# The compression of keys and values in steps beside the projection columns of the second block's attention

## The reference

```python
parts = jnp.split(h @ w_kv, 6, axis=-1)           # kc, vc, ks, vs, kw, vw: 4 groups x 64 each
kc, ks, kw = rope(kc, pos), rope(ks, pos), rope(kw, pos)
def compress(t, pe, w1, w2):                      # 15 blocks of 32 tokens, stride 16
    blk = t[:, cidx] + pe[None, None, :, None, :]
    blk = blk.transpose(0, 3, 1, 2, 4).reshape(B, G, n_cmp, CMP_LEN * dh)
    return jax.nn.gelu(blk @ w1) @ w2             # w1: 2048 x 256, w2: 256 x 64
k_cmp = compress(kc, cmp_pe_k, cmp_k_w1, cmp_k_w2)
v_cmp = compress(vc, cmp_pe_v, cmp_v_w1, cmp_v_w2)
proj = h @ w_in                                   # queries 1024 columns, gates 48
```

## Time and profile before

| | |
|---|---|
| median of three runs | 1549.62 us |
| profiled execution, its own time | 1545.94 us |
| span of its trace | 1544.1 us |
| PE busy | 1411.0 us (91%) |
| DVE busy | 1151.0 us (75%) |
| ACT busy | 930.5 us (60%) |
| chain that ended last | PE 75%, DVE 12%, DMA 5%, ACT 4%, issue 3% |

### The profile page before, as it was taken

The page is one execution under the profiler, slowest core; times in us unless marked ns, Lnnn a source line. Parts: engine busy times, 40 slices in busy tenths (PEclk is TensorE's granted clock), DMA queues, the critical chain, the costliest instruction groups (busy, mean ns, idle before and its releaser), DMA issues.

```text
span 1544.1 us, 18883 instructions
## 1 busy us (share of the span) xinstructions
PE 1411.0 (91%) x7388; PEld 1181.8 (77%) x7388; DVE 1151.0 (75%) x1371; ACT 930.5 (60%) x1094; POOL 77.8 (5%) x80
## 2 busy tenths in 40 slices
PE   6999996999999696799699999996999999699998
PEld 5877875888888585577578888875778887599986
DVE  4775658999999766377689999987567456558772
ACT  4454535989988434055389999873555654445561
POOL 0000000000000000000100000000276000000000
PEclk9999997999999797799699999998999999899999
DMA  9554544999999446200479999993544433545551
GB/s 330 175 163 137 191 163 149 376 388 384 385 400 394 170 142 204 74 1 1 150 266 385 390 386 385 410 375 117 171 141 159 164 137 110 176 149 182 189 178 41
DMA packets 127277, 343.15 MB, mean 222 GB/s; under 512 B 8956, under 2 KB 15692, under 8 KB 110668
## 3 DMA queue, kind: packets, MB, share of 16 engines
q1 hardware_dynamic: 117472, 327.37, 58.4%
q10 hardware_dynamic: 9708, 14.47, 2.9%
HBM read 340.77 MB, written 1.05 MB: 221 GB/s over the span
## 4 chain that ended last, share of the span: by engine, by line
PE 75%; DVE 12%; DMA 5%; ACT 4%; issue 3%; PEldq 1%; PEld 1%; ACTq 0%; DVEq 0%
PE PS L619 24%; PE PS L1248 15%; PE PS L500 8%; PE PS L576 6%; PE PS L556 4%; DVE wlo L467 4%; DMA raw<-in_moe_w_down 2%; PE PS L1287 2%; PE PS L1237 2%; ACT whi L461 2%; DMA raw<-in_moe_w_gate 2%; PE PS L1322 2%; PE PS L1318 1%; PE PS L2016 1%; PE PS L702 1%
## 5 line engine op out<-in xcount | busy, mean ns | idle before, releaser
L467 DVE TENSOR_TENSOR wlo<-raw,whi 128x2048 fp32r<-128x2048 f32 x314 | 707.6, 2277 | 123.8 <-ACT whi L461 118.5
L461 ACT ACTIVATE whi<-raw 128x2048 fp32r<-128x2048 f32 x314 | 589.4, 1897 | 32.0 <-PE PS L556 17.3
L619 PE MATMUL PS<-whi,th 128*128 128x512 f32 (+1 forms) x544 | 217.9, 401 | 6.9 <-DVE tl L717 6.9
L619 PE MATMUL PS<-whi,tl 128*128 128x512 f32 (+1 forms) x544 | 215.9, 397 | 0.0
L619 PE MATMUL PS<-wlo,th 128*128 128x512 f32 (+1 forms) x544 | 214.5, 394 | 0.0
L1248 PE MATMUL PS<-whi,xg 128*128 128x512 f32 x512 | 205.6, 402 | 0.0
L1248 PE MATMUL PS<-wlo,xg 128*128 128x512 f32 x512 | 200.5, 392 | 0.0
L619 PEld LDWEIGHTS PS<-whi,th 128*128 128x128 f32 x544 | 103.7, 191 | 32.4 <-DVE tl L717 7.9
L619 PEld LDWEIGHTS PS<-wlo,th 128*128 128x128 f32 x544 | 103.9, 191 | 23.8
L619 PEld LDWEIGHTS PS<-whi,tl 128*128 128x128 f32 x544 | 103.6, 190 | 23.7
L1248 PEld LDWEIGHTS PS<-whi,xg 128*128 128x128 f32 x512 | 96.4, 188 | 18.6
(11 more groups left out here) (401 smaller groups left out, 2284.2 us busy)
## 6 DMA issues: line engine op xcount, KB each, us to landing
raw<-in_moe_w_gate SPq DMA_DIRECT2D x64, 1024.0 KB, 7.6
raw<-in_moe_w_up SPq DMA_DIRECT2D x64, 1024.0 KB, 8.5
raw<-in_moe_w_down SPq DMA_DIRECT2D x64, 1024.0 KB, 7.9
raw<-in_w_in SPq DMA_DIRECT2D x32, 1024.0 KB, 5.2
raw<-in_ret_w_in SPq DMA_DIRECT2D x24, 1024.0 KB, 5.2
raw<-in_w_up SPq DMA_DIRECT2D x20, 1024.0 KB, 5.1
raw<-in_w_down SPq DMA_DIRECT2D x10, 1024.0 KB, 5.0
raw<-in_ret_w_out SPq DMA_DIRECT2D x8, 1024.0 KB, 5.0
```

Of the source, the lines that this page charges most:

```text
L461: nc.scalar.activation(s.whi[:, high, 0:kc, 0:wide], s.raw[:, slot, 0:kc, 0:wide], ACT.Copy).then_inc(s.hi_done, 1)
L467: nc.vector.tensor_tensor(s.wlo[:, slot, 0:kc, 0:wide], s.raw[:, slot, 0:kc, 0:wide], s.whi[:, high, 0:kc, 0:wide], ALU.subtract).then_inc ...
L619: last = nc.tensor.matmul(PS[:, 2 * (col % 2) + tt, 0:wide], x[:, KC * kb + c, tt * P:(tt + 1) * P], w[:, k, c, 0:wide], start=(kb == 0 an ...
```

## The change

`l_nsa_in` is cut into two query columns (`l_nsa_q`) and a gate column (`l_nsa_g`). Between them stand four new blocks of the ring: the first compression weights, 1024 rows by 256 columns each, loaded by SyncE and used unsplit (ScalarE and VectorE only pass the semaphores on). Sixteen steps stand behind the blocks: 0 to 5 behind keys and values, 6 to 9 behind queries, 10 to 13 behind the compression blocks, 14 and 15 behind the gate blocks. Every column is rotated as soon as it is copied out. The doubled copy goes: VectorE's adds read the transposed tokens in PSUM banks 5 and 6, the lower or upper half of the partitions, and write either half of `cmp_x`. The small compression weights are loaded, in seven transfers issued by ScalarE, ahead of the projection, and GpSimd instead of VectorE sets the zero parts of `n_kp` and `n_vp`. Of the stage ends only the last stays.

```diff
-        l_nsa_in = linear(3, [4, 4], plain(a["nsa_w_in"][0]))
+        l_nsa_q = linear(2, [4, 4], plain(a["nsa_w_in"][0]))
+        cmp_b0 = blocks[0]
+        blocks[0] += 4
+        l_nsa_g = linear(1, [4, 4], plain(a["nsa_w_in"][0], 2 * BW))
...
+        def cmp_sync(sp):
+
+            for i in range(4):
+                b = cmp_b0 + i
+                src = a["cmp_k_w1" if i < 2 else "cmp_v_w1"][D * (i % 2):D * (i % 2) + D, :]
+                sp.wait_ge(block_used, b - RAWS + 1)
+                sp.dma_start(cmp_block(i), src.rearrange("(c p) n -> p c n", p=P)).then_inc(raw_ready[b % RAWS], 16)
+
+        def nsa_split_hi(act, s, b, turn, kc=KC, wide=BW):
+            if cmp_b0 <= b < cmp_b0 + 4:
+                act.wait_ge(raw_ready[b % RAWS], ready_value(s, b, 0))
+                act.drain().then_inc(hi_done, 1)
+            else:
+                split_hi(act, s, b, 0, KC, 3 * NSA_H if l_nsa_g.b0 <= b < l_nsa_g.b0 + 2 else BW)
...
+        def nsa_beside_tensor(pe, n):
+
+            half = CMP_LEN // 2
+            if n == 2:
+                pe.wait_ge(cmp_loaded, 7 * 16)
+                for k in range(2):
+                    for b in range(2):
+                        last = nc.tensor.transpose(PS[:, 4, (2 * k + b) * half:(2 * k + b + 1) * half],
+                                                   cmp_pe[0:half, k, b].rearrange("p a d -> p (a d)"),
+                                                   cst[0:half, C_ID:C_ID + half])
+                last.then_inc(cmp_turned, 1)
+            if n == 3:
+                pe.wait_ge(rotated, ROTATED_KC)
+                for k in range(2):
+                    nsa_turn_tensor(lambda tt: n_kvc[:, tt, :], 256 * k, 5 + k).then_inc(cmp_turned, 1)
+            if n == 7:
+                pe.wait_ge(rotated, ROTATED_KW)
+                pe.wait_ge(cmp_built, BUILT_PE)
+                nsa_turn_tensor(lambda tt: n_k[:, tt, :], 0, 7).then_inc(cmp_turned, 1)
+                nsa_turn_tensor(lambda tt: n_k[:, tt, :], 256, 4).then_inc(cmp_turned, 1)
+            if n == 9:
+                pe.wait_ge(rotated, ROTATED_Q0)
+                pe.wait_ge(cmp_built, BUILT_V)
+                for i in range(2):
+                    last = nsa_turn_tensor(lambda tt: n_q[:, 0, tt, :], 256 * i, 5 + i)
+                last.then_inc(cmp_turned, 1)
+            if n in (12, 14):
+                k = n // 2 - 6
+                pe.wait_ge(cmp_copied, COPIED_GV if k else COPIED_GK)
+                for c in range(2):
+                    last = nc.tensor.transpose(PS[:, 4 if k else 7, 256 + c * 64:256 + c * 64 + 60],
+                                               cmp_g[0:60, k, c * P:(c + 1) * P], cst[0:60, C_ID:C_ID + 60])
+                last.then_inc(cmp_turned, 1)
+            if n == 12:
+                pe.wait_ge(rotated, ROTATED_Q1)
+                pe.wait_ge(cmp_copied, COPIED_Q0)
+                for i in range(2):
+                    last = nsa_turn_tensor(lambda tt: n_q[:, 1, tt, :], 256 * i, 5 + i)
+                last.then_inc(cmp_turned, 1)
+            if n == 13:
+                pe.wait_ge(cmp_built, BUILT_H)
+                for c in range(2):
+                    last = nc.tensor.matmul(PS[:, 7, 384:444], cmp_w2k[:, c, :, :].rearrange("p b d -> p (b d)"),
+                                            cmp_h[:, c, :], start=(c == 0), stop=(c == 1))
+                last.then_inc(cmp_turned, 1)
+            if n == 15:
+                pe.wait_ge(cmp_built, BUILT_HR)
+                for g in range(NSA_G):
+                    for c in range(2):
+                        last = nc.tensor.matmul(PS[0:60, 4, g * NSA_DH:(g + 1) * NSA_DH],
+                                                cmp_hr[:, c, g].rearrange("p r n -> p (r n)"), cmp_w2v[:, c, :],
+                                                start=(c == 0), stop=(c == 1))
+                last.then_inc(cmp_turned, 1)
...
+        def nsa_in_tensor(pe):
+
+            steady_tensor(pe, l_nsa_kv, th, tl, lambda n: nsa_beside_tensor(pe, n))
+            steady_tensor(pe, l_nsa_q, th, tl, lambda n: nsa_beside_tensor(pe, 6 + n))
+            for i in range(4):
+                k = i // 2
+                pe.wait_ge(lo_done, cmp_b0 + i + 1)
+                if i % 2 == 0:
+                    pe.wait_ge(cmp_built, BUILT_KW if k else BUILT_KS)
+                for c in range(8):
+                    last = nc.tensor.matmul(PS[0:60, 4 if k else 7, 0:CMP_HID], cmp_x[:, k, 8 * (i % 2) + c, 0:60],
+                                            cmp_block(i)[:, c, :], start=(i % 2 == 0 and c == 0),
+                                            stop=(i % 2 == 1 and c == 7))
+                last.then_inc(block_used, 1)
+                nsa_beside_tensor(pe, 10 + i)
+            steady_tensor(pe, l_nsa_g, th, tl, lambda n: nsa_beside_tensor(pe, 14 + n))
...
+            if n in (9, 12):
+                j = n // 12
+                act.wait_ge(cmp_turned, (CMP_Q0, CMP_Q1)[j])
+                for i in range(2):
+                    last = nc.scalar.activation(n_qT[:, 4 * j + 2 * i:4 * j + 2 * i + 2, :].rearrange("p c t -> p (c t)"),
+                                                PS[:, 5 + i, :], ACT.Copy)
+                last.then_inc(cmp_copied, 1)
+            if n in (11, 13):
+                k = n // 13
+                act.wait_ge(block_used, cmp_b0 + 2 * k + 2)
+                nc.scalar.activation(cmp_g[0:60, k, :], PS[0:60, 4 if k else 7, 0:CMP_HID],
+                                     ACT.Gelu_apprx_tanh).then_inc(cmp_copied, 1)
...
+        def cmp_build_vector(dve, o, k):
+
+            dve.wait_ge(cmp_turned, (CMP_K, CMP_V)[k])
+            for g in range(NSA_G):
+                rows = slice(64 * (g % 2), 64 * (g % 2) + 64)
+                tokens = PS[rows, 5 + k, SEQ * (g // 2):SEQ * (g // 2) + SEQ].rearrange("p (i s b) -> p s i b", s=8, b=2)
+                for b in range(2):
+                    for h in range(2):
+                        o(nc.vector.tensor_tensor(
+                            cmp_x[64 * b:64 * b + 64, k, 8 * h:8 * h + 8, 15 * g:15 * g + 15], tokens[:, :, h:h + 15, b],
+                            cmp_peT[rows, k, b, 8 * h:8 * h + 8].unsqueeze(2).broadcast_to([64, 8, 15]), ALU.add))
+            o.wait()
+            hand(dve, cmp_built)
+
+        def nsa_beside_vector(dve, o, n):
+
+            if n == 2:
+                dve.wait_ge(cmp_turned, CMP_PE)
+                o.then(nc.vector.tensor_copy(cmp_peT[:, :, :, :].rearrange("p k b s -> p (k b s)"),
+                                             PS[:, 4, 0:2 * CMP_LEN]))
+                hand(dve, cmp_built)
+                o(nc.vector.memset(n_ckp[:, :, :, :], 0.0))
+            if n in (3, 4):
+                cmp_build_vector(dve, o, n - 3)
+            if n == 7:
+                for seg, bank in enumerate((7, 4)):
+                    dve.wait_ge(cmp_copied, (COPIED_KS, COPIED_KW)[seg])
+                    pair = PS[:, bank, :].rearrange("p (c t) -> p c t", c=2)
                     for half in range(2):
...
+        def nsa_rotated(dve, o, l, j, x, heads):
+
+            dve.wait_ge(acc_free, 2 * (l.n0 + j + 1))
+            nsa_rotate(dve, o, x, heads)
+            o.wait()
+            hand(dve, rotated)
+
+        def nsa_in_vector(dve, o):
+
+            def rotate_keys(j):
+                nsa_rotated(dve, o, l_nsa_kv, j, n_kvc if j == 0 else n_k[:, :, 256 * (j - 1):256 * j], 4)
+
+            def rotate_queries(j):
+                nsa_rotated(dve, o, l_nsa_q, j, n_q[:, j], 8)
+
+            def gates_of(j):
+                dve.wait_ge(acc_free, 2 * (l_nsa_g.n0 + 1))
+                nsa_gates_vector(dve, o)
+            steady_side(dve, l_nsa_kv, nsa_split_lo, rotate_keys, lambda n: nsa_beside_vector(dve, o, n))
+            steady_side(dve, l_nsa_q, nsa_split_lo, rotate_queries, lambda n: nsa_beside_vector(dve, o, 6 + n))
+            for i in range(4):
+                nsa_split_lo(dve, sweep_first, cmp_b0 + i + AHEAD, 0)
+                nsa_beside_vector(dve, o, 10 + i)
+            steady_side(dve, l_nsa_g, nsa_split_lo, gates_of, lambda n: nsa_beside_vector(dve, o, 14 + n))
...
+        def cmp_params():
+
+            w2k = a["cmp_k_w2"].rearrange("(c p) d -> p c d", p=P)
+            return [(cmp_pe[0:CMP_LEN // 2, k, :, i, :], a[n].rearrange("(s b) d -> s b d", b=2))
+                    for k, n in enumerate(("cmp_pe_k", "cmp_pe_v")) for i in range(2)] + [
+                (cmp_w2k[:, :, 0, :], w2k), (cmp_w2k[:, :, 1, :], w2k),
+                (cmp_w2v[:, :, :], a["cmp_v_w2"].rearrange("(c p) d -> p c d", p=P))]
...
+                if layer == 0:
+                    pool.wait_ge(normed, 4)
+                    for b in range(2):
+                        o.then(nc.gpsimd.memset(n_kp[64 * b:64 * b + 64, :, :, 1 - b, :], 0.0))
+                    for side in (0, 2):
+                        o.then(nc.gpsimd.memset(n_vp[:, :, :, :, side, :], 0.0))
+                    pool.drain().then_inc(pool_steps, 1)
```

(40 more changed lines are left out.)

275 lines of the change are left out of this document (77 added, 198 removed).

## The result

The changed kernel took 1523.23 us (median of 4 executions, 1517.76 to 1526.32) against 1547.94 before (4 executions, the three shown above among them, 1545.36 to 1552.52): ratio 0.984, 95% interval 0.980 to 0.987. The forecast was 1523, its range 1515 to 1535. The profiled execution took 1521.7 with a span of 1519.9 us; the span before was 1544.1, so the two traces differ by 24.2 us. The changed kernel's trace starts its first projection matmul at 530.62 instead of 531.90, so distances are compared, not times on the axis. My measure is the distance from the first projection matmul of this stage to the first compressed-key score matmul, with which attention opens. Before it was 646.02 - 531.90 = 114.1; now it is 619.96 - 530.62 = 89.3. The gain of 24.8 us lies within this stretch.

A forecast was written before the change was run, and what follows sets the result against it. TensorE, three quarters of the chain, stood still or did serial work for 49.7 us before attention; 21.7 + 0.9 + 2.4 + 1.5 less 0.9 makes 25.6, a gain of 24.1 us. Forecast 1523, range 1515 to 1535 with rivals.

The forecast's parts named there:

- TensorE's added work: Transposes, compression matmuls and small products between projection and attention, none overlapping a projection: 21.7 us on TensorE's path.
- VectorE, first half: Rotations, side-building adds and splits beside keys, values and first queries: TensorE waits 0.9 us, 4 us with slow adds.
- VectorE, second half: From the split of b9 through query rotation and compression: VectorE keeps ahead; the 7.81 and 14.08 us idle stretches go.
- The sign that I named for the first half: In the new profile, the only wait on a split stands ahead of the block after the first query block.
- Tail: Gate blocks and last products: TensorE ends at 618.0, the ScalarE-to-VectorE chain at 620.4, costing 2.4 us beyond TensorE.
- Hand-overs: Some eleven places where TensorE waits on a semaphore add 0.1 to 0.2 us each: 1.5 us in all.
- Edits at nothing: Early small-weight loads on ScalarE (3.5 to 11 us, hidden) and zeroing moved to GpSimd: taken as zero.
- Cold start of attention: Attention's first matmuls, 7.04 us at clock 0.50 before, would again start at 0.50.
- Rival (b): TensorE enters attention at full clock, so the first 7.04 us cost 3.5 and next products 1 less: 1518.5; 9%.
- Downstream: After attention's start nothing takes the gain back: the ring is full in both, the experts' stream begins later by the same amount.
- Rival (d): Attention's start moves but the stream of the experts ends as before: 1548; 3%.
- Rival (c): Eleven small pieces in TensorE's stream each cost 2.2 us wait and 2.2 us clock, 48 us: 1572, slower; 3%.

The follow-up runs named there:

- second trace: The changed kernel run once more, unaltered, beside the same runs of the kernel before: 1521.56 us (5 executions), ratio 0.985.
- the fourth experiment: Kernel before, with the value side's 16 additions reading PSUM while the key side's still read SBUF: 1545.77 us in one execution.
- the gate's blocks set apart: Changed kernel with the first gate block between the compression's two sides and the second behind its last block: 1525.8 us in one execution.
- the turned gate product: Changed kernel, gate weights standing and tokens moving, gate before compression, second query column's transposes moved, first scores ahead of the stage's end: 1516.12 us, ratio 0.980.
- each addition twice: Changed kernel with each of VectorE's 32 adds issued a second time into a spare tile: 1527.16 us for the whole execution.
- queries turned at the end: Changed kernel with the queries' 16 transposes and four evictions put back behind the last product: 1516.69 us for the whole.

## Why the prediction was right

The direction, the place and the size were right: 24.1 us forecast, 24.8 measured in the stretch and 24.2 in the span. That the median came within 0.3 us of the 1523 is luck: the changed kernel's executions lie 8.6 us apart, and its second trace has a gain of 27.7 in the stretch. By its steps:

- *TensorE's added work*, forecast 21.7: the chain has four groups of large transposes in 0.87 + 0.87 + 0.87 + 1.03 = 3.6 (forecast 4.7), compression 10.50 + 3.59 = 14.1 (14.2), transposes behind the gelu 0.65, small products 0.58 and 1.91 (0.66 and 1.10), the position transposes 0.35: 21.2 in all. 0.9 of it is slow clock, in the last transposes and the last product (told under the tail), so the work is 20.3 at full clock, 1.4 under the forecast. 1.1 of that is the large transposes: I took the 1.17 us that a group of 8 shows by itself, and in a full stream it adds 0.87.
- *VectorE, first half*, forecast a wait of 0.9 us: there was none. The term that failed is the price of an addition. I took SBUF's price, with the earlier trace rows on 512-column operations as the nearest row, and bounded it only upward (0.1 us more). The small strided form is 68 ns cheaper with an input in PSUM, shown by the fourth experiment: 5.1 - 4.0 = 1.1 us a side, which is the forecast wait and a little slack.
- *VectorE, second half*, no wait: right. The sign that I named for the first half, one wait on a split, did not show either.
- *Tail*: the last product was forecast to end at 618.0 on the old axis, 616.7 on the new; it ended at 618.62. The missing term is the clock. I priced the narrow blocks at full clock although had it falling after 4 us of such a column. It fell 2.6 us in and cost 2.6 in the second block and 0.8 in the last product; 1.6 of this was won back by reaching the tail early. Beyond TensorE the stage then took 1.3 us, not 2.4: the slow blocks hid the chain from ScalarE to VectorE, as the gate's blocks set apart showed by laying it bare.
- *Hand-overs*, forecast 1.5: PE's busy time equals every stretch up to 607.85, so next to nothing of it is seen (what is left when all pieces are added up is 0.2). Forecast for tail, wait and hand-overs together 4.8, measured 1.35 of idle time and 3.4 of lost clock: the total was right partly because errors met, the work and the waits too dear, the clock left out.
- *Edits at nothing*: the seven loads of small weights took ScalarE from 529.25 to 533.64, 4.4 us, between my ends of 3.5 and 11, and hidden. The zeroing cost VectorE nothing: the last two subtractions ahead of the first projection, beside GpSimd's first memsets (527.24 to 530.9), took 0.69 us each, as before the change, and the split behind them 2.28. The rows from which I took the price of GpSimd's company I read on one engine only: in the kernel before, a split from 1112.14 took 2.60 instead of 2.29, but GpSimd's four operations beside it took 4.76 us, and 2.84 with no split beside them. The larger part fell on GpSimd.
- *Cold start of attention* at 0.50: as forecast. Rival (b) gave 3.5 us for a warm one, and the turned gate product showed it can be had: the scores took 3.8.
- *Downstream*: from the first score to the end it is 898.1 us before and 899.9 and 898.3 in the changed kernel's two traces, so the gain is kept to the end within 2 us. Rival (d) is refuted.
- *Rival (c)* charged each late hand-over 2.2 us of wait and 2.2 of clock. It did not happen here, and its price for the clock was an upper end: the late hand-over in the turned kernel cost 2.2 + 1.6, and of the two late splits with each addition twice one cost 2.0 + 0 and the other 3.7 + 2.0.

## What to carry to other kernels

A serial chain of small steps costs its sum only while nothing else stands on TensorE; strewn between the blocks of a projection whose engine never waits, it costs its TensorE time and what the clock takes (21 us of work, 25 with all, of 50 here). A block that becomes shorter or moves uncovers what it hid: look up, for each engine, what is queued ahead of the short operation that TensorE will ask for, and put the hand-over that is already ready before the long one. Where a product has few output columns, let its weights stand and the tokens move: the gate took 2.8 us so and 0.25 for turning its result back, against 5.3 at full clock and 7.9 as it ran.

## What the runs showed of the hardware

- A strided 64x120 addition on VectorE took 345 ns with both inputs in SBUF and 277 with one in PSUM, though 128x512 operations show no difference.
- A matmul over 48 moving columns came every 0.111 us and one over 256 every 0.117, at full clock (changed kernel and turned gate).
- The clock fell while TensorE was never idle, in a run of 48-column matmuls: 2.6 us into it in one execution of the changed kernel and about 5 in the other, and not within a single block of 2.79 us between wide matmuls. Attention's first scores, 30 columns each, began at 0.50 or fell to it in every trace but the two with the turned gate.
- It fell also behind a wait of 2.2 us in a busy stretch, and the 16 matmuls behind it took 5.23 us instead of 3.59; behind a wait of 2.0 us (each addition twice) it did not. With 128x128 transposes alone on TensorE it came back from 0.50 (0.56 over 3.3 us of them, 1.00 in the 1.2 us behind them; queries turned at the end), as it did before the change.
- The Trainium skill (TensorE: Matmul & The Clock Gate, "Part 4: PE-mode transpose") says that transposes do not count as work for the clock gate; the two stretches just named do not agree with it.
